# First modulation of a two-layer trunk kernel: another order of loads, weight pieces and vector products

## The reference, cut to what matters

```python
cond = jax.nn.silu(c)
for layer in range(DEPTH):
    shift, scale, gate = jnp.split((cond @ w_ada[layer] + b_ada[layer])[:, None, :], 3, axis=-1)
    h = rms_norm(x, norm_g[layer]) * (1.0 + scale) + shift
    (qkv_a, z_a, beta_raw, alpha_raw, glu_in, z_b, ...) = split_columns(h @ w_in[layer])
    ...
    x = x + gate * (merged @ w_out[layer])
```

## Time and profile before

| what | value |
|---|---|
| median of 3 runs | 2201.28 us (2201.27 to 2202.84) |
| profiled execution | 2204.61 us |
| its span, first to last instruction | 2202.8 us |
| PE busy | 2141.9 us, 97% of the span |
| POOL busy | 1664.1 us, 76% |
| DVE busy | 1226.9 us, 56% |
| ACT busy | 959.8 us, 44% |
| DMA | 479.58 MB, mean 218 GB/s |

### The profile page before, as it was taken

How to read it: one execution, slowest core, us unless ns; L and a number is a source line. 1 busy time by engine, 2 the same in 40 slices (tenths; PEclk the granted TensorE clock), 3 DMA queues, 4 the chain that set the end, 5 groups by cost and what they waited for, 6 DMA issues and landing times.

```text
span 2202.8 us, 37773 instructions
## 1 busy us (share of the span) xinstructions
PE 2141.9 (97%) x14842; PEld 1950.5 (89%) x14842; DVE 1226.9 (56%) x2153; ACT 959.8 (44%) x1056; POOL 1664.1 (76%) x676
## 2 busy tenths in 40 slices
PE   5899999999999999999989999999999999999999
PEld 3799999988889988788989999999788999888899
DVE  6959874857555454535562894656667445430110
ACT  3344444483333534444344444446533354444442
POOL 1568768766765898988868885877767679898876
PEclk8899999999999999999999999999999999999999
DMA  9976535444443699898965664554445358966654
GB/s 374 400 254 230 179 125 182 163 134 161 160 156 113 226 340 332 303 339 321 360 236 182 195 212 144 164 165 151 158 144 162 129 182 318 340 205 204 228 184 153
DMA packets 122202, 479.58 MB, mean 218 GB/s; under 512 B 13360, under 2 KB 17712, under 8 KB 109392
## 3 DMA queue, kind: packets, MB, share of 16 engines
q1 hardware_dynamic: 121904, 477.54, 62.1%
q10 hardware_dynamic: 160, 0.13, 0.0%
HBM read 471.19 MB, written 6.29 MB: 217 GB/s over the span
## 4 chain that ended last, share of the span: by engine, by line
PE 42%; POOL 30%; issue 23%; DVE 3%; ACT 1%; DVEq 1%; POOLq 0%; ACTq 0%; DMA 0%
POOL wl L536 30%; PE ps L937 13%; PE ps L938 13%; PE ps L939 13%; DVE score L1629 1%; ACT wh L557 0%; PE ps L1299 0%; POOLq L535 0%; PE ps L1306 0%; PE ps L1287 0%; PE ps L1233 0%; ACTq L734 0%; PE ps L1222 0%; PE ps L1255 0%; PE ps L1249 0%
## 5 line engine op out<-in xcount | busy, mean ns | idle before, releaser
L536 POOL TENSOR_TENSOR wl<-raw,wh 128x1024 fp32r<-128x1024 f32 x672 | 1663.9, 2489 | 525.7 <-ACT wh L557 523.8
L557 ACT CAST wh<-raw 128x1024 fp32r<-128x1024 f32 x672 | 703.7, 1050 | 1111.8 <-PE ps L939 861.8
L937 PE MATMUL ps<-ah,wh 128*128 128x256 f32 x3008 | 868.2, 289 | 20.4 <-DVE al L1499 14.1
L938 PE MATMUL ps<-al,wh 128*128 128x256 f32 x3008 | 856.7, 285 | 0.0
L939 PE MATMUL ps<-ah,wl 128*128 128x256 f32 x3008 | 856.4, 285 | 0.0
L937 PEld LDWEIGHTS ps<-ah,wh 128*128 128x128 f32 x3008 | 583.5, 194 | 27.1 <-DVE al L1499 14.4
L938 PEld LDWEIGHTS ps<-al,wh 128*128 128x128 f32 x3008 | 583.4, 194 | 4.2 <-issue 3.9
L939 PEld LDWEIGHTS ps<-ah,wl 128*128 128x128 f32 x3008 | 583.0, 194 | 0.0
L937 PE MATMUL ps<-wh,ah 128*128 128x512 f32 (+1 forms) x832 | 319.9, 384 | 0.9 <-POOL wl L536 0.9
L939 PE MATMUL ps<-wh,al 128*128 128x512 f32 (+1 forms) x832 | 317.2, 381 | 0.0
L938 PE MATMUL ps<-wl,ah 128*128 128x512 f32 (+1 forms) x832 | 317.0, 381 | 0.0
(11 more groups left out here) (280 smaller groups left out, 1705.2 us busy)
## 6 DMA issues: line engine op xcount, KB each, us to landing
raw<-w_piece SPq DMA_DIRECT2D x672, 512.0 KB, 3.4
modw<-w_ada SPq DMA_DIRECT2D x64, 1024.0 KB, 7.9
adaw<-w_first SPq DMA_DIRECT2D x32, 1024.0 KB, 8.3
gbias<-b_gate SPq DMA_DIRECT2D x24, 256.0 KB, 3.9
xs<-xt SPq DMA_DIRECT2D x2, 2048.0 KB, 12.9
skew<-stage SPq DMA_DIRECT2D x8, 256.0 KB, 4.6
bias<-skew SPq DMA_DIRECT2D x2, 1024.0 KB, 8.2
x<-xs SPq DMA_DIRECT2D x4, 512.0 KB, 6.2
```

What stands on the lines that cost most here:

```text
L536: nc.gpsimd.tensor_tensor(wl[:, s], raw[:, s], wh[:, s].bitcast(F32), ALU.subtract).then_inc(sem("w_split"), 1)
L557: A.copy(wh[:, s], raw[:, s]).then_inc(sem("w_rounded"), 1)
L937: M.matmul(o, lh, rh, start=start, stop=False, skip_group_check=True)
L938: M.matmul(o, lh, rr, start=False, stop=False, skip_group_check=True)
```

## The change

Four things change, all in layer 0's first modulation. No instruction is added or removed, except that products of two blocks write elsewhere.

- SP: loads 0 to 7 go out with nothing between them. `x` and the parameters go behind load 7. The first 18 pieces have new places: 0 and 1 behind load 9, 2 and 3 behind load 10, then one each behind loads 12, 13, 15, 16, 17, 18, 20, 21, 23, 24, 25, 26, 28, 29.
- DVE: the sixteen products of quarter 0 are taken without a break, then the first six of quarter 1, and only then the reciprocal and the normalised quarter 0. After quarter 0's `al` one product of quarter 1 follows as before, but now it is the seventh.
- `ADA_SIDE` is 0, 6, 2, 2 for the four quarters: six blocks of quarter 1 are summed in `acc`.
- ACT: two pieces are rounded ahead of `h_high(0)` and four behind it. Quarters 1 to 3 keep their counts.

```diff
-        ADA_SIDE = 2
+        ADA_SIDE = (0, 6, 2, 2)
+        CHUNKS_BEHIND = {9: (0, 1), 10: (2, 3), 12: (4,), 13: (5,), 15: (6,), 16: (7,), 17: (8,), 18: (9,), 20: (10,),
+                         21: (11,), 23: (12,), 24: (13,), 25: (14,), 26: (15,), 28: (16,), 29: (17,)}
...
-                if n == 2:
+                if n == 7:
                     sp.dma_start(xs[:], xt.rearrange("p (k t) -> p k t", t=T)).then_inc(sem("x_landed"), 16)
...
-                        for i, at in ((5, 10), (4, 9), (3, 7), (2, 6), (1, 4), (0, 2)):
-                            if n >= at and (n - at) % 8 == 0 and n - at < 24:
-                                chunk(6 * ((n - at) // 8) + i)
+                        for i in CHUNKS_BEHIND.get(n, ()):
+                            chunk(i)
...
-                    for q in range(3):
-                        rounds(hc, RING, hc % RING)
+                    for q, early in ((0, 2), (1, RING), (2, RING)):
+                        rounds(hc, early, hc % RING)
                         h_high(q)
-                        rounds(hc + RING, 2, (hc + RING) % RING)
+                        rounds(hc + early, 6 - early, (hc + early) % RING)
...
-                    ahead = ADA_SIDE if q else 0
+                    ahead = ADA_SIDE[q]
...
                     for q in range(4):
+                        if q:
+                            normed_quarter(q)
+                        ada_part(q, ADA_SIDE[q] + 1 if q else 0, KT)
+                        if q < 3:
+                            ada_part(q + 1, 0, ADA_SIDE[q + 1])
                         if q == 0:
-                            ada_part(0, 0, 10)
                             normed_x()
-                        normed_quarter(q)
-                        ada_part(q, ADA_SIDE + 1 if q else 10, KT)
-                        if q == 0:
+                            normed_quarter(0)
                             dve.wait_ge(sem("par_landed"), 16)
                             dve.wait_ge(sem("con_landed"), 16)
-                        if q < 3:
-                            ada_part(q + 1, 0, ADA_SIDE)
                         quarter_mods(q)
```

More of the change, by code:

```diff
@@ L1528, in _ @@
                         if q < 3:
-                            ada_part(q + 1, ADA_SIDE, ADA_SIDE + 1)
+                            ada_part(q + 1, ADA_SIDE[q + 1], ADA_SIDE[q + 1] + 1)
                 def products(n):
```

## The result

The changed kernel is slower: median 2212.79 us (2206.16 to 2214.51, 6 runs) against 2201.47 us (2200.46 to 2203.78, 6 runs) of the kernel before on the same chip. The ratio over all runs is 1.0044, 95% interval 1.0033 to 1.0055 (the two medians alone give 1.0051). The forecast had the sign and the place, and too little of the size: 2206.7 us, at most 2209.8. The profiled execution took 2206.16 us. It is the fastest of its six, and experiment 8 deals with that.

A forecast was written before the change was run, and what follows sets the result against it. PE is busy 97%, so only the start counts, paced by DVE with a full DMA queue. Quarter 2's late `h_high(2)` passes 5.4 us on: 2201.28 + 5.4 = 2206.7 us, range 2203.3 to 2209.8.

The forecast's parts named there:

- The sixteen products: DVE, quarter 0: products run without starving and end at 29.4 us, 13 us gained.
- `mods(0)` within 0.7 us: DVE, quarter 0: `mods(0)` was to start at 49.3 us instead of 46.28, quarter 0 starting 3.0 us later.
- `h_high(1)` and `h_high(2)` behind pieces 9 and 15: ACT: `h_high(1)` at 76.9 us, 1.4 late, behind piece 9's rounding; `h_high(2)` at 108.4, 5.1 late (5.4 taken), behind piece 15's.
- quarter 3 without a new wait for `h_high`: Quarter 3: no further load is late; load 31 lands at 125.6 us, and DVE wants it at 129.0.
- the shift passing on to the end: DVE and PE wait for `h_high(2)`, so 5.4 us pass to `mods(3)`, PE's last start and the end.
- the rivals: Faster queue 2203.6 us (0.07); head start survives 2198.9 (0.05), 2196.3 (0.03); second stall 2210.5 (0.08); stall not passed on 2203 (0.02).
- The 1.1 us: DVE, quarter 1's fifth and sixth products beside POOL: 1.1 us more for one product, bounds 0 and 1.65.
- The stream of quarter 2: DMA queue behind load 21: loads 22 to 26 and pieces 11 to 15 take 18.8 us, piece 15 landing at 107.4.

The follow-up runs named there:

- experiment 8: The changed kernel run again unaltered for a second profile: 2210.25 us against 2202.82 us for the kernel before, ratio 1.0036.
- experiments 1 and 6: Changed kernel, ACT rounding two pieces (1: 2206.86 us) or one (6: 2205.03 us) ahead of the high halves; 6 also in the kernel before: 2223.74 us.

## Why the prediction was wrong in size and right in place

**Right.** The sixteen products, `mods(0)` within 0.7 us, `h_high(1)` and `h_high(2)` behind pieces 9 and 15, quarter 3 without a new wait for `h_high`, and the shift passing on to the end. None of the rivals came true. The text said that it would be wrong if `h_high(2)` were released by DVE; it was released by the piece.

That `mods(0)` came so near is partly luck. The fifth and sixth product took 1.93 us more than the two before them (4.57 against 2.64), not 1.1, and the normalised quarter took 1.36 us, not 2.58. The 1.1 us rested on a misreading as well: the trace before has the product with two operands in SBUF not only at 2048 elements but three times at 1024, 1.28 us each, with POOL idle. What it lacks is that form beside POOL.

**The step that failed: the sizes along the chain.** The last start was to be 131.5 + 5.4 = 136.9; it was 140.9. The 3.9 us are four terms, and the first three came again in the second profile of the changed kernel (13.89, 7.75 and 20.48 us for the spans below):

- *`h_high(1)`, +0.7.* `mods(0)` came 0.65 us sooner than I said, load 15 landed at 62.9 instead of 63.4. But pieces 6 to 9 and loads 16 to 18 took 13.75 us from there (62.90 to 76.65), not 12.55.
- *From `h_high(1)` to load 21's issue, +0.84.* I took the 6.90 us of the kernel before. The trace after has 7.74, because `al` took 2.54 us instead of 1.29 (it also started 0.40 us sooner behind `h_high(1)`): POOL began to split piece 9 at 77.79, 0.95 us before it. I had seen that piece 9 would be rounded just ahead of `h_high(1)`, and not that POOL is therefore always at work when `al` comes. `gsc` (1.81 instead of 0.16) met the same, without cost, since ACT waited for the piece.
- *The stream of quarter 2, +1.15.* "5 x 2.49 + 5 x 1.27 = 18.8", with 19.1 taken; measured 20.25 us, from 90.18 (load 21, again 4.8 us after its issue, as in the earlier trace rows) to 110.43.
- *From `h_high(2)` to the last start, +1.22.* `al` at 112.53 is 2.54 us long again, with POOL on piece 15 from 111.58: PE starts 3.11 us after `h_high(2)` instead of 2.26. Another 0.37 us pass until `mods(3)`.

POOL's rows and the second `al`; where no piece is split beside it, in experiments 1 and 6, `al` takes 1.29 us again:

```profile
77.79 2.34 POOL L537 TENSOR_TENSOR wl<-raw,wh 128x1024 fp32r<-128x1024 f32 x1 [2.21 <-ACT wh L558]
...
111.58 2.34 POOL L537 TENSOR_TENSOR wl<-raw,wh 128x1024 fp32r<-128x1024 f32 x1 [1.43 <-ACT wh L558]
```

```profile
112.53 2.54 DVE L1500 TENSOR_TENSOR al<-xs,ah 128x512 fp32r<-128x512 f32 x2 [4.61 <-ACT ah L598]
```

The stream's error is instructive. The DMA view of the changed kernel from 90.3 to 110.3 us (mean rate; queue q8 carries the program's code; the share is of 16 engines):

```profile
DMA packets 1462, 8.36 MB, mean 418 GB/s; under 512 B 160, under 2 KB 160, under 8 KB 725
...
q8 instruction: 1, 0.02, 0.3%
```

The rate was as assumed, 418 GB/s over 20 us. But 8.36 MB passed, and loads 22 to 26 with pieces 11 to 15 are 7.86 MB. The other 0.5 MB, 1.2 us, belongs to transfers behind piece 15. The trace's completion events say how that can be: each transfer has sixteen, and it counts as landed at the last. Fifteen of piece 15's came by 109.48 us, the sixteenth at 110.44; fifteen of piece 9's by 75.49, the sixteenth at 76.65. Up to the fifteenth the two streams took 19.3 and 12.6 us, as forecast (19.1 and 12.55). So what both sums missed is one part in sixteen that lags, while the others go on to the next transfers. A bytes-over-rate sum gives when the bytes could be there, not when a given piece is. What held that part back is argued, not shown: one packet of 16 KB of code falls in each such stream. Here, from 98.0 to 99.5 us:

```profile
q8 instruction: 1, 0.02, 4.0%
```

4.0% of 16 engines in 1.5 us is 0.96 us of one engine. The sixteenth event is at most 0.11 us behind the fifteenth up to load 23, 0.50 us behind at piece 12, which lands just before the packet, and 0.93 to 0.96 us behind for each transfer after it until the queue runs dry. Both kernels have such a packet in each quarter (before at 53.7, 75.0, 94.9 and 117.3 us), with landings up to 1.4 us late behind it. The delay is not the same behind each, and no run took a packet away.

**From the start to the end.** The profile's +9.3 us and the medians' +11.3 and +7.4 us in two sets of runs are of one size, since the second profile's start was 11.5 us late. The range ended at +8.5; its upper bound rested on the DMA rate and on `mods(0)`, and held no term for contention on `al`.

**The Trainium skill** ("SBUF — State Buffer", section "Who interferes with whom") came closer than my term at one place: a sixth product blocked for a whole POOL operation would have cost 0.4 us more than the 1.1 I took, and the measured 1.93 us lie beyond both. For `mods(0)` as a whole it came out further off (49.7 against my 49.3, measured 48.65), since the normalised quarter was hardly held. The same rule, that such two-input instructions contend with GpSimd's reads, holds one instruction further, for `al`, `gsc` and the next normalised quarter; the rows (2.54, 1.81, 3.23 us) agree with it.

## What to carry to other kernels

Where one engine's queue mixes a critical step with the preparation of data that arrives by DMA, write down for each critical step the last transfer ahead of it, and where that stands in the DMA queue: both orders are one setting. The other direction counts as well: a transfer that waits for a slot holds every transfer behind it, so an earlier place in the DMA queue needs an earlier consumer, and two edits that each cure a stall can together make a larger one. Price the steps after a late arrival with what that arrival sets off on the other engines, not with their durations from the undisturbed profile.

## What the runs showed of the hardware

- A DVE operation with two operands in SBUF that comes while POOL is in its own operation is held, however small it is: `gsc` on 128x4 elements took 1.81 us beside POOL and 0.16 alone, `al` 2.54 and 1.29, a normalised quarter 3.23 and 1.23. The products that sum in PSUM kept 1.29 us beside POOL.
- The opening product of a quarter, with one tensor operand and its result in SBUF, is held too. It takes 0.75 us alone (at 33.33 us in the profile after); beside POOL's operation of 69.09 to 71.48 us it took:

```profile
69.20 2.83 DVE L1425 TENSOR_SCALAR acc<-adaw,cond 128x1024 f32<-128x1024 f32 x1 [0.19 <-issue]
```

- PE's stretches at 1.2 GHz, with PE busy throughout, come and go between executions. The one near 280 us (3.2 us) is in one of the changed kernel's two profiles and not in the other; one near 1345 us (1.6 us) is in the kernel before and in neither of these. Two single profiles ended 1.6 us apart where the starts were 9.3 us apart.
- One of the sixteen parts of a transfer can land 0.95 to 1.4 us behind the other fifteen in a busy queue, and the transfer with it; for load 21, the first after the queue had run dry, the sixteenth was 0.08 us behind.
